# Experts' weights issued from GpSimd's queue, in one order with the gathers, and four result buffers

## Reference

```python
logits = xf @ w_router + b_router            # 512 tokens, 32 experts
top_val, top_idx = top_k(logits, 4)
gates = softmax(top_val)
# for each expert e, over the tokens that chose it:
hu = x @ w_up[e] + b_up[e]                   # 1024 -> 2048
act = glu * sigmoid(1.702 * glu) * (lin + 1) # clipped halves of hu
y = act @ w_down[e] + b_down[e]              # 1024 -> 1024
out[token] += gate * y
```

## Time and profile before

| | |
|---|---|
| time before, median of 3 runs | 2974.77 us (2969.39 to 2980.22) |
| span of the profiled execution | 2972.9 us |
| PE busy in the span | 2791.1 us (94%) |
| up-products of the experts, line 1853 | 565.1 us |
| down-products of the experts, line 1891 | 248.5 us |
| bytes moved, all DMA | 648.31 MB, mean 218 GB/s |
| weight loads of the experts' passes | 186 of 2048 KB, and six for the overflow block |

### The profile page before, as it was taken

One profiled execution on the slowest core, in us unless ns is written; L12 is line 12 of the kernel. 1 busy time (PEld: TensorE's weight loads), 2 busy tenths in 40 slices (PEclk: granted clock), 3 DMA queues, 4 the chain that ended last, 5 costly groups with the idle time before them and its releaser, 6 DMA issues.

```text
span 2972.9 us, 37665 instructions
## 1 busy us (share of the span) xinstructions
PE 2791.1 (94%) x15911; PEld 1383.8 (47%) x15911; DVE 1137.4 (38%) x1440; ACT 465.5 (16%) x916; POOL 242.0 (8%) x369
## 2 busy tenths in 40 slices
PE   7998889898899989999999999999999999999998
PEld 3446775532223322333333465477654334556773
DVE  3855553511111111121124253455436663444544
ACT  1112142000000000000001143000023662200001
POOL 1000011111111011101011500000000110000000
PEclk9998989899999999999999999999999999999999
DMA  9775234899999999999999131213132223221310
GB/s 340 283 255 227 100 115 163 332 358 403 391 393 395 410 408 409 407 407 407 410 413 363 31 111 64 77 67 113 57 73 56 60 63 113 106 85 57 113 57 28
DMA packets 172883, 648.31 MB, mean 218 GB/s; under 512 B 75965, under 2 KB 77573, under 8 KB 140305
## 3 DMA queue, kind: packets, MB, share of 16 engines
q1 hardware_dynamic: 156674, 607.76, 53.3%
q0 software_dynamic: 15984, 38.18, 4.1%
q10 hardware_dynamic: 64, 0.07, 0.0%
HBM read 626.49 MB, written 24.06 MB: 219 GB/s over the span
## 4 chain that ended last, share of the span: by engine, by line
PE 77%; DMA 14%; DVE 4%; issue 2%; ACT 1%; DVEq 1%; SPq 0%; ACTq 0%; POOL 0%; POOLq 0%
PE ps L1853 14%; PE ps L2534 10%; PE ps L2569 10%; DMA slots<-in_w_down_dram 8%; PE ps L1891 8%; PE ps L2872 4%; PE ps L2605 4%; PE ps L2243 3%; PE ps L3128 2%; DMA slots<-in_ada_w_dram 2%; PE ps L1899 2%; PE ps L2499 2%; PE ps L2416 2%; PE ps L2519 2%; PE ps L1245 2%
## 5 line engine op out<-in xcount | busy, mean ns | idle before, releaser
L1853 PE MATMUL ps<-slots,hT 128*32 128x512 f32 x5120 | 565.1, 599 | 11.9 <-DMA slots<-in_w_up_dram 10.8
L1853 PEld LDWEIGHTS ps<-slots,hT 128*32 128x32 f32 x5120 | 165.7, 111 | 386.5 <-issue 364.6
L2569 PE MATMUL ps<-slots,work 128*128 128x512 f32 x672 | 289.6, 592 | 2.8 <-DVE work L2647 2.8
L1891 PE MATMUL ps<-slots,work 128*32 128x512 f32 x2112 | 248.5, 614 | 45.6 <-DMA slots<-in_w_down_dram 45.2
L2006 DVE TENSOR_SCALAR stage<-ps 128x512 f32<-128x512 f32 (+1 forms) x47 | 32.3, 686 | 547.0 <-PE ps L1857 546.6
L2569 PEld LDWEIGHTS ps<-slots,work 128*128 128x128 f32 x672 | 127.5, 190 | 162.5 <-issue 157.8
L2534 PE MATMUL ps<-hT,slots 128*128 128x256 f32 x768 | 168.7, 379 | 0.0
L1891 PEld LDWEIGHTS ps<-slots,work 128*32 128x32 f32 x2112 | 70.9, 112 | 192.8 <-issue 187.0
L2872 PE MATMUL ps<-hT,slots 128*128 128x512 f32 x352 | 156.8, 601 | 0.0
L2534 PEld LDWEIGHTS ps<-hT,slots 128*128 128x128 f32 x768 | 145.9, 190 | 22.4 <-issue 2.9
L2744 DVE TENSOR_TENSOR work<-work,ps 128x1024 f32<-128x1024 f32 x60 | 71.6, 1219 | 165.1 <-PE ps L2569 164.9
(11 more groups left out here) (611 smaller groups left out, 3506.1 us busy)
## 6 DMA issues: line engine op xcount, KB each, us to landing
slots<-in_w_up_dram SPq DMA_DIRECT2D x128, 2048.0 KB, 20.4
slots<-in_w_down_dram SPq DMA_DIRECT2D x64, 2048.0 KB, 19.1
slots<-in_mlp_w_dram SPq DMA_DIRECT2D x32, 2048.0 KB, 7.9
slots<-in_ada_w_dram SPq DMA_DIRECT2D x40, 1024.0 KB, 5.0
slots<-in_w_ada_dram SPq DMA_DIRECT2D x16, 1024.0 KB, 5.5
slots<-in_w_in_dram SPq DMA_DIRECT2D x5, 2048.0 KB, 15.8
slots<-in_rnn_w_in_dram SPq DMA_DIRECT2D x24, 384.0 KB, 4.2
slots<-in_w_ada_dram SPq DMA_DIRECT2D x4, 2048.0 KB, 18.5
```

The lines of the kernel that those rows point to most:

```text
L1853: ins = pe.matmul(to, x[:, k, unit * UNIT:(unit + 1) * UNIT], upw[s][:, k % 2, col:col + CH], start=k == 0, stop=False)
L1891: ins = pe.matmul(to, actT[:, 4 * q + j, 64 * u + 32 * h:64 * u + 32 * h + 32], downw[sl[h]][:, j, half * CH:(half + 1) * CH], start=k == ...
L2569: ins = pe.matmul(ps[:, bank + t], x[:, k, t * P:(t + 1) * P], w[:, k], start=k == 0, stop=k == HK - 1)
```

## The change

SP no longer loads the weights of the passes; it only counts them, and keeps the overflow block's loads. GpSimd issues them, as `moe_load`, each behind a wait for its slot, with semaphores `moe_landed` of their own. They stand in one order with gathers and result writes: in pass i the up-loads of pass i + 1, list entries, the gather of pass i + 4, the down-loads of pass i, and the result writes of pass i - 1. `settle` still stands ahead of each gather and each result write. There are four result buffers in place of two; the two new ones lie in `work`. The list and the gather of the overflow block are issued at other places. Besides that, some semaphores are merged under one name with higher counts (not shown, apart from one).

```diff
@@ constants_sp
-                sp.dma_start(t, A["k_" + name]).then_inc(S("constants"), 16)
+                sp.dma_start(t, A["k_" + name]).then_inc(S("rows_moved"), 16)
@@ result buffers
-        gbuf, lbuf, sbuf_, ybuf = (t[:].rearrange("p (b n) -> p b n", b=2) for t in (stage, tmp, modA, modB))
+        gbuf, lbuf, sbuf_ = (t[:].rearrange("p (b n) -> p b n", b=2) for t in (stage, tmp, modA))
+        NY = 4
+        ybuf = [modB[:, 0:CH], modB[:, CH:2 * CH], work[:, 8192:8704], work[:, 8704:9216]]
@@ moe_sp
+        moe_loads = [0] * 6
+        moe_landed = [S(f"moe_landed{i}") for i in range(6)]
+        moe_freed = [S(f"freed{i}") for i in range(6)]
+
+        def moe_load(g, s, src, dst):
+            g.wait_ge(moe_freed[s], moe_loads[s])
+            g.dma_start(dst, src).then_inc(moe_landed[s], 16)
+            moe_loads[s] += 1
+
+        def up_loads(g, i, js):
+            e = g.value_load(tab[0:1, RANKS[i]:RANKS[i] + 1], min_val=0, max_val=E - 1)
+            for j in js:
+                moe_load(g, up_slot[i][j], moe_up_w(e, j), up_rows[up_slot[i][j]])
+
+        def down_loads(g, i):
+            e = g.value_load(tab[0:1, RANKS[i]:RANKS[i] + 1], min_val=0, max_val=E - 1)
+            for j, s in enumerate(down_slot[i]):
+                moe_load(g, s, moe_down_w(e, j), down_rows[s])
 
         def moe_sp(sp):
-            sp.wait_ge(S("route_step"), ROUTE["table"])
-            for i in range(NPASS + 1):
-                if i < NPASS:
-                    e = sp.value_load(tab[0:1, RANKS[i]:RANKS[i] + 1], min_val=0, max_val=E - 1)
-                    for j, s in enumerate(up_slot[i]):
-                        load(sp, s, moe_up_w(e, j), up_rows[s])
-                if i:
-                    e = sp.value_load(tab[0:1, RANKS[i - 1]:RANKS[i - 1] + 1], min_val=0, max_val=E - 1)
-                    for j, s in enumerate(down_slot[i - 1]):
-                        load(sp, s, moe_down_w(e, j), down_rows[s])
+            moe_loads[:] = loads
+            for i in range(NPASS):
+                for s in up_slot[i] + down_slot[i]:
+                    loads[s] += 1
             sp.wait_ge(S("route_step"), ROUTE["blocks"])
@@ moe_pool
             g.memset(tick[:], 0.0)
             g.drain()
+            g.wait_ge(S("route_step"), ROUTE["table"])
+            up_loads(g, 0, range(4))
             g.wait_ge(S("route_step"), ROUTE["rows"])
             g.wait_ge(S("h2_out"), 16 * TT)
             g.wait_ge(S("block_y"), 64)
             moe_gather(g, 0)
+            up_loads(g, 1, (0, 1))
             g.wait_ge(S("route_step"), ROUTE["biases"])
             moe_gather(g, 1)
+            up_loads(g, 1, (2, 3))
             g.wait_ge(S("route_step"), ROUTE["listed"])
             moe_gather(g, 2)
+            down_loads(g, 0)
             g.wait_ge(S("route_step"), ROUTE["blocks"])
             moe_gather(g, 3)
             g.wait_ge(S("list_filled"), 16)
-            for i in range(NPASS):
+            for i in range(NPASS + 1):
+                if 0 < i < NPASS - 1:
+                    up_loads(g, i + 1, range(4))
                 for j in range(2 * i, min(2 * i + 2, TT * TOPK)):
                     g.indirect_dma_start(list_dram, bass.IndirectOffsetOnAxis(ap=sloti[:, j:j + 1], axis=0),
                                          pairs[:, LCOLS * j:LCOLS * (j + 1)], None, bounds_check=E * T - 1, oob_is_err=False).then_inc(S("list_out"), 16)
                 if i + 4 < NPASS:
                     moe_gather(g, i + 4)
-                for q, units, at in quads(i):
-                    d, n = up_piece[i] + q, units * 2 * UNIT
-                    g.wait_ge(S("y_ready"), d + 1)
-                    settle(g)
-                    g.indirect_dma_start(y2_dram, bass.IndirectOffsetOnAxis(ap=ysl[0:n, at:at + 1], axis=0), ybuf[0:n, d % 2], None,
-                                         bounds_check=2 * T * TOPK - 1, oob_is_err=False).then_inc(S(f"y_out{d % 2}"), 16)
-                if i == NPASS - 4:
+                if i == NPASS - 7:
                     g.wait_ge(S("list_out"), 16 * TT * TOPK)
                     block_list(g, 0, 0)
+                if i == NPASS - 4:
                     g.wait_ge(S("xg_free"), NPASS - 3)
                     g.wait_ge(S("block_list"), 80)
                     block_gather(g)
+                if 0 < i < NPASS:
+                    down_loads(g, i)
+                if i:
+                    for q, units, at in quads(i - 1):
+                        d, n = up_piece[i - 1] + q, units * 2 * UNIT
+                        g.wait_ge(S("y_ready"), d + 1)
+                        settle(g)
+                        g.indirect_dma_start(y2_dram, bass.IndirectOffsetOnAxis(ap=ysl[0:n, at:at + 1], axis=0), ybuf[d % NY][0:n], None,
+                                             bounds_check=2 * T * TOPK - 1, oob_is_err=False).then_inc(S(f"y_out{d % NY}"), 16)
@@ moe_pe, up: and the same for the three waits of down
-                        take(pe, s)
+                        moe_take(s)
@@ moe_dve, y_out
-                    if d >= 2:
-                        v.wait_ge(S(f"y_out{d % 2}"), 16 * (d // 2))
-                    bank = ps[:, down_banks[i][q]]
+                    if d >= NY:
+                        v.wait_ge(S(f"y_out{d % NY}"), 16 * (d // NY))
+                    bank, y = ps[:, down_banks[i][q]], ybuf[d % NY]
```

More of the change, by code:

```diff
@@ L287, in ada_first_act @@
             a.copy(ada_c, cT[:].unsqueeze(3).broadcast_to([P, 2, KT, 32]))
-            a.drain().then_inc(S("c_silu"), 1)
+            a.drain().then_inc(S("act_made"), 1)
             rms_scales_act(a, "1")
@@ L471, in rms_scales_dve @@
         def rms_scales_dve(v, key):
-            v.wait_ge(S("x_in"), 16)
+            v.wait_ge(S("tile_in"), 16)
             for t in range(TT):
@@ L1456, in route_act @@
                 a.activation(gates[:, t * 4:t * 4 + 4], top[:, t, 0:4], ACT.Exp, bias=small[:, t:t + 1], accum_out=small[:, 8 + t:9 + t])
-            a.drain().then_inc(S("gate_exp"), 1)
+            a.drain().then_inc(S("act_made"), 1)
         def route_dve(v):
@@ L1719, in moe_sp @@
             sp.wait_ge(freed[0], nb + loads[0])
-            for p in range(2):
-                sp.wait_ge(S(f"y_out{p}"), 16 * ((UPS + 1 - p) // 2))
+            for p in range(NY):
+                sp.wait_ge(S(f"y_out{p}"), y_outs(p))
             sp.wait_ge(S("block_done"), nb)
-            sp.dma_start(ycomb[0], y_tiles[0]).then_inc(S("comb_in"), 16)
+            sp.dma_start(ycomb[0], y_tiles[0]).then_inc(S("tile_in"), 16)
             for t in range(3):
@@ L1814, in moe_pool, with moe_take @@
                 g.wait_ge(S("block_x"), b * 16 + 32)
-            for p in range(2):
-                g.wait_ge(S(f"y_out{p}"), 16 * ((UPS + 1 - p) // 2))
+            for p in range(NY):
+                g.wait_ge(S(f"y_out{p}"), y_outs(p))
         def moe_pe(pe):
             came = [0] * 4
+            came_in = [0] * 6
+            def moe_take(s):
+                came_in[s] += 16
+                pe.wait_ge(moe_landed[s], came_in[s])
             def turn_x(i):
@@ L1877, in down @@
                 sl = down_slot[i]
-                take(pe, sl[0])
+                moe_take(sl[0])
                 if UNITS[rank] % 2:
-                    take(pe, sl[1])
+                    moe_take(sl[1])
                 for k in range(KT + 1):
                     if k == 4 and UNITS[rank] % 2 == 0:
-                        take(pe, sl[1])
+                        moe_take(sl[1])
                     for q, two, at in quads(i):
@@ L2525, in hidden @@
             def hidden(b):
-                read, copied = before("hid_read", key) - 6, before("hid_copied", key) - 1
+                read, copied = before("hid_read", key) - 6, before("act_made", key) - 1
                 sums = before("mlp_sum", key) + 9 - 12
@@ L3139, in out_sp @@
                 sp.wait_ge(S("x_done"), 4 + t + 1)
-                sp.dma_start(out[0, t * P:(t + 1) * P], X[:, t]).then_inc(S("written"), 16)
-            sp.wait_ge(S("written"), 16 * TT)
+                sp.dma_start(out[0, t * P:(t + 1) * P], X[:, t]).then_inc(S("rows_moved"), 16)
+            sp.wait_ge(S("rows_moved"), N_CONST + 16 * TT)
         def reached(sp, n):
```

70 lines of the change are left out of this document (36 added, 34 removed), and 2 rows, old and new, of the table OTHER.

## The result

The changed kernel takes **3322.85 us** (median of 4 runs, 3310.51 to 3327.64). The kernel before, run beside it on the same chip, takes 2977.49 us. The ratio is **1.1156, 95% interval 1.1126 to 1.1186**: about 345 us slower. The profiled execution has a span of 3318.8 us (2972.9 before).

What follows compares the result with a forecast made beforehand. Transfers bound the expert stage, with a saturated DMA queue and TensorE 7 us behind per pair of passes. 265 + 105 + 10 - 10 + 5 = 375 us on 2974.8 gave 3350 us, range 3265 to 3450.

Steps and rivals of the forecast that it cites:

- The row that decides: GpSimd's issue waits of 8 and 17 us: its drain waits until everything GpSimd issued before has landed.
- What the drain costs: Expert stage: 78 empty queues at 3.4 us, 265; 105 behind small transfers; 10 for extra gathers; 10 taken off.
- the part that is hidden: Two passes with six and five units, whose long TensorE work absorbs some of the gaps: 10 us taken off.
- the overflow block's loads stay on SP: Overflow block: its loads keep their queue and wait for the same slots, so they add 0.
- The small transfers: Behind drains, loads wait for a gather or first write: queue empty another 1.7 us, 62 times, 105 us.
- the move itself: 186 weight loads from SP to GpSimd: issue beside transfers, same bytes and transfer time; only the first gather 5 us later.
- Start: Stage start: the first gather waits for the first four loads until 552 and lands 5 us later.
- Faster: Expert stage: plain loads don't hold the drain and one ring is quicker, 425 GB/s, so 2939 us; chance 0.03.
- No change: Expert stage: drains pass over loads and the rate stays, 2975 to 2983 us; chance 0.04.
- TensorE's clock: TensorE stays at its lower clock after waits, a pair needing 109 us, so 3660 us, much slower; chance 0.04.
- The signs: Mid-stage: DMA share about 0.72, some 300 GB/s, issue waits 10 to 25 us, weight waits in hundreds, pair 85 to 93.

Runs made afterwards that it cites:

- experiment 2: Changed kernel with the add and drain left out ahead of the passes' gathers and result writes (78 places), loads still on GpSimd: 3012.63 us, ratio 1.0125.
- experiment 7: Changed kernel without drains in the passes and also without the one ahead of the overflow block's first gather: 3014.05 us, ratio 1.0108.
- experiment 1: Changed kernel with the passes' weight loads issued from SP again, order, four buffers, drains and renamed semaphores kept: 2979.68 us, ratio 1.0005.
- The fourth experiment: Changed kernel with one more add and drain ahead of the up-loads of each pass (29 added): 3408.3 us, ratio 1.1426.
- experiment 3: Changed kernel with one drain per pass, behind all six loads, in place of two or three: 3189.25 us, ratio 1.0710.

## Why the prediction was right

I said 3350 us, range 3265 to 3450; measured was 3322.85. I said +375, measured is +345.

**The row that decides** held. I read from two delays of 8 and 17 us that the drain waits for landings, and assumed the same for plain loads. The runs show it: waits of 2.4, 13, 22 and 31 us behind a small write alone, two, four and six loads, and over the whole trace of the kernel after each ends 0.84 to 1.36 us after the last landing (0.6 to 2.0 in the traces of the other kernels with drains). I had taken 0.86, which is what it is behind a small transfer (0.84 to 0.89); behind loads the median is 1.03.

**What the drain costs.** Of the 370 us that I had for drains (265 + 105 + 10 - 10, bounds 252 to 479), they take 307. A pair in the middle of the stage takes 87.7 us, I said 89, but that holds a part that isn't the drains'. The start of VectorE's first read of each up-product (line 2006 before; line 2040 after, line 2038 in experiment 2) says how far each kernel is in each pass. Experiment 2 has the loads on GpSimd and no drains in the passes, so the last column is what drains do; its router ended 8 us later than that of the kernel after, so only the growth of the column counts.

| pass | units | before, us | exp. 2, us | after, us | after less before | after less exp. 2 |
|---|---|---|---|---|---|---|
| 0 | 2 | 572.2 | 582.5 | 579.7 | 7.4 | -2.8 |
| 2 | 6 | 645.7 | 655.8 | 662.2 | 16.6 | 6.4 |
| 6 | 5 | 772.2 | 784.7 | 830.4 | 58.1 | 45.7 |
| 13 | 4 | 1004.5 | 1016.0 | 1131.3 | 126.8 | 115.3 |
| 15 | 3 | 1065.0 | 1076.5 | 1210.4 | 145.4 | 133.9 |
| 28 | 3 | 1485.5 | 1508.1 | 1782.4 | 296.9 | 274.3 |
| 30 | 3 | 1547.2 | 1580.7 | 1863.2 | 316.0 | 282.5 |

From pass 15 to 28 the drains cost 10.8 us a pass, where my sum had 12.3 (380 us before the part that is hidden, over 31 passes). So their price was some 1.5 us a pass too high, 46 us in all: the term of the sum that was mis-sized most. From pass 0 to 15 they cost 9.1 a pass. There stand the passes with four, five and six units, in which TensorE is busy for longer, so it fits that gaps cost less there; no run tests it. Fifteen passes at 1.7 us less make 25 us, where I took off 10.

**The end of the stage: a term that I put at nothing.** I wrote that the overflow block's loads stay on SP: 0. After the start of pass 30 the kernel after loses another 30 us. TensorE waits 18.3 us for one down-load of the last pass, which GpSimd issues only at 1883.6, behind two result writes with their drains, while SP issues the overflow block's up-loads from 1857.8 on. Without any drain (experiment 7) the same wait is 7.0 us, and with all loads on SP (experiment 1) there is none. The last pass's down-loads use two slots of `w_up` (line 1688 of the kernel before), unlike those of all other passes: that down-loads always fall on the slots of the down-loads before holds only up to pass 29. So they start late in any case, and in these kernels another queue's loads run beside them.

**The small transfers.** I gave 1.7 us of empty queue behind each gather or first write. In the timeline above the loads start right after the gather's own 0.96 us (1425.08 to 1426.04), so reading the expert's number costs nothing that can be seen; I had taken 0.4. (The parts that I gave for the 1.7 make 1.63, and I derived its bounds from nothing.) The fourth experiment prices a drain without a small transfer behind it at 2.8 us where I had 3.4, the others a drain with one at 3.9 where I had up to 5.1. All within my bounds, at their lower side. By the Trainium skill, "DMA: Bandwidth & Descriptors", section "Anatomy of one DMA — SWDGE (gpsimd) path", the sum would have been 43 us less, an estimate of 3307: 16 us under the measured time, where mine is 27 over it. No run here shows its fixed part by itself.

**One queue's own cost: the step that was missing.** I gave the move itself only 5 us, for the first gather. The runs give 35. The traces of experiments 1 and 2, whose spans differ by 38.5 us, say where. About 2 us are there at pass 0: from the first gather's issue to TensorE's start on it pass 13.8 us in experiment 2, 10.7 in experiment 1, 9.8 before. From pass 0 to pass 28 come 17.6 us (12.4 against the kernel before); they fit the rate, 397 GB/s for 407, which over all of the stage's 410 MB would make 25. The last 19 us come behind the start of pass 28, and as many in experiment 7, which has no drain there. Of them 5 and 7 us are the two kernels' waits for the last pass's down-load; the rest isn't shown. So errors of opposite sign met: drains 63 us too dear, the move itself 30 us too cheap, and 375 - 345 is what is left. The mechanism was right; that the forecast came within 1% owes something to luck.

**Start.** I said that the first gather waits until 552 and that x is there 5 us later. It was issued at 552.21, after 13.4 us of "issue"; TensorE began at 558.03 in place of 551.78, and that with a router that was 2.3 us ahead in this execution: 8.5 us, where I had 5.

**The rivals.** "Faster" fell: the drain passes over nothing, and one queue is slower, not quicker. "No change" fell with it: experiments 1 and 2 speak against it twice, 345 us with drains and 35 without. By the Trainium skill, "DMA: Bandwidth & Descriptors", section "Issuing engines are not separate DMA queues", issuing from several engines saves issue time only; these two measurements differ from that. "TensorE's clock" was seen but in the small: 61 us of longer products, always followed by a wait for weights. After 11.15 us of waiting, eight matmuls take 1.93 us at a granted clock of 0.50, the lower level, 1.2 GHz; 6.8 us later forty take 4.48 at 1.00, the higher one, as in the earlier trace rows:

```profile
1438.81 1.93 PE L1925 MATMUL ps<-slots,work 128*32 128x512 f32 x8 [11.15 <-DMA slots<-in_w_down_dram]
...
1445.58 4.48 PE L1925 MATMUL ps<-slots,work 128*32 128x512 f32 x40
```

**The signs** I named came: DMA share 0.73 to 0.74 (I said 0.72), 293 to 299 GB/s (300), waits called "issue" of 13 and 22 us, TensorE's waits for weights 340 us (hundreds), a pair 87.7 us (85 to 93). The stages behind kept their length: from the last result write to the end pass 1371.8 us, 1367.3 before.

**Open.** Why weights issued from GpSimd move at 2% less at the same DMA share, where the rest of the last 19 us comes from, and why one of experiment 3's drains costs 4.8 us in place of 3.9.

## What to carry to other kernels

Before transfers are moved to another queue, look for what on that engine waits for landings. Here a drain ahead of small transfers was free as long as the engine's queue held nothing large, and cost an empty queue each time once it did (3.9 us each, 78 times); the same 78 drains beside a queue kept full from another engine were worth nothing. The length of the wait says little: 30 us of waiting cost 3.9, because what is waited for has to be moved anyway; count the stretches with nothing queued, in a fine slicing of the DMA row. And look at the end of the stage, where what stays on the old queue meets what has moved.

## What was not expected of the hardware

- Weights issued from GpSimd alone moved at 397 GB/s over 500 us, from SP alone at 407, with a third on SP at 402, all with the DMA engines busy for the whole time (share 1.00 to 1.01).
- Price per drain was the same, 3.9 us, whether it stood ahead of a gather or of a write, and the halves added up to the whole within 5 us.
- A second queue beside the drained one gave back only 0.7 us of 3.9: in the stretch shown, both were empty at the same time.
- The next issue came 0.84 to 1.36 us after the last landing at each of 69 drains, whether the wait had been 2 us or 22.
